# Second product with gathers: GpSimd's low parts start after the next group's weights, and VectorE's order is changed with them

## The chip, the cores and the metric

One NeuronCore of a Trainium2 chip runs the whole program. The engines are TensorE (PE), VectorE (DVE), ScalarE (ACT), GpSimd (POOL) and SyncE (SP, which only issues DMAs here). The metric is the device time of one execution in microseconds; lower is better.

## The reference, cut to what matters

The program is a two-layer block (attention and gated linear attention, then a recurrent layer), each layer followed by a PEER layer, a mixture of 16384 one-row experts. The change lies in the PEER layer of layer 0, in its last product.

```python
def peer_ffn(h, wq, k1, k2, u, v):
    ...                                   # scores, top 16 of 128 x 128 experts for each of 8 heads
    idx = jnp.take_along_axis(cand_i, pos, axis=-1)
    g = jax.nn.softmax(top_s, axis=-1).astype(h.dtype)
    def block(args):
        hb, ib, gb = args
        ue = jnp.take(u, ib, axis=0)
        ve = jnp.take(v, ib, axis=0)
        act = jax.nn.gelu(jnp.einsum('td,thkd->thk', hb, ue), approximate=False)
        return jnp.einsum('thk,thkd->td', gb * act, ve)
    out = lax.map(block, ...)             # 6 tiles of 128 tokens in layer 0, D = 1024
```

## The kernel before, in words

For 5 of the 6 tiles of 128 tokens in layer 0 the kernel does not gather: it has computed the activation of every expert for every token (`acts`) and a sparse matrix of gate values (`gates`), and the output is the dense product (acts * gates) times the table `peer_v`, 16384 rows by 1024 columns. The 6th tile is done with gathers: its 128 chosen rows of `peer_u` and of `peer_v` per token are fetched by indirect DMAs, multiplied and summed on VectorE. `combine_with_gathers` does both at once.

**Groups.** The table is cut into 128 slots of 128 rows, and four slots make a group (`GC = 4`, `NG = 32` groups). A group makes 10 **pieces** on TensorE (`NP = 10`: 5 tiles by 2 halves of 512 columns), each 12 matmuls: 4 slots by 3 products, since each operand is split into a high and a low fp16 part (`vh`, `vl` of the table, `wh`, `wl` of the weights) and the product of the two low parts is left out. The high and low buffers exist twice (index `q`), the loaded fp32 buffers `vr`, `gr`, `ar` once per slot `x` of a group. The result of a piece goes to one of 4 PSUM banks, and VectorE adds it into `ACC`; piece y + 4 may start when piece y has been added (`added`).

**The engines in a group.** All of it is one period per group g, in which the operands of group g + 1 are made while TensorE works on group g.
- VectorE (`period`, L1695) runs through the 10 pieces: for each the addition into `ACC` (L1700), and behind it what a table of numbers assigns to that piece (L1539): `weigh_at` the four products `ar = ar * gr` of group g + 1 (L1668), `low_at` the four subtractions `wl = ar - wh` of group g + 1 (L1673), `dot_at` the four row products with `ug` for the gathered tile (L1680), and `sum_at` the four additions of gathered rows `vg` into the PSUM tensor `sum_ps` (L1692), ahead of them `set_share` (L1685).
- ScalarE makes `vh` (L1626) from `vr` and `wh` (L1628) from `ar`, in the order vh0, wh0, vh1, wh1 and so on, then one gelu.
- GpSimd (`period`, L1593) makes the four `vl = vr - vh` of group g + 1 (L1591, function `low`), then issues four gathers of `ug` and four of `vg` (L1585), each when VectorE has finished with the buffer (`dotted`, `summed`).
- SyncE (L1576 to L1579) loads, slot by slot in this fixed order: `gr` and `ar` when `wl` of that slot of the group before is made (`w_cut`), then `vr` when its `vl` is made (`v_cut`). It waits at each step, so a later slot's loads stand behind an earlier slot's waits.
- TensorE (L1659) starts a group when its four `vl` (`v_cut`) and its four `wl` (`w_cut`) are made.

The operands of VectorE matter here. L1668 and L1673 read two tensors in SBUF, and so does the small L1685. L1700, L1680 and L1692 read one in SBUF and one in PSUM (`ex_R`, `hp`, `sum_ps`).

The function next door for layer 1 (`combine_experts`, matmuls on L1486) has no gathers, 8 PSUM banks and 8 pieces, and is not touched.

Of the kernel before, what the change touches and what calls it, by code (L numbers as in the profile page):

```python
# [1525 lines left out]
def combine_with_gathers(nc, io, gates, acts, chosen_rows, chosen_gates, HS, ACC, layer, first_tile):  # L1526
# [4 lines left out]
    GC = 4  # L1531
# [4 lines left out]
    SLOTS = PH * PTOP // NG  # L1536
    assert 2 * NP % BANKS == 0
    if NP == 10:
        weigh_at, low_at, dot_at, sum_at = (0, 0, 1, 1), (3, 3, 4, 4), (2, 2, 5, 5), (7, 8, 8, 9)  # L1539
    else:  # L1540
        weigh_at, low_at, dot_at, sum_at = (0, 0, 0, 0), (2, 2, 2, 2), (1, 1, 3, 3), (4, 4, 5, 5)
    with ExitStack() as c:
# [19 lines left out]
        with signals(nc, *names) as sems:  # L1562
# [6 lines left out]
            with nc.Block() as block:  # L1569
                @block.sync  # L1570
                def _(sp):
                    with sp.Fori(0, NG) as g:
                        for x in range(GC):
                            s = g * GC + x
                            sp.wait_ge(w_cut, s + 1)
                            sp.dma_start(gr[x][:, :], gates[bass.ds(s, 1), :, c0:c0 + NT].rearrange("o p t -> p (o t)")).then_inc(g_in[x], 16)  # L1576
                            sp.dma_start(ar[x][:, :], acts[bass.ds(s, 1), :, 0:NT].rearrange("o p t -> p (o t)")).then_inc(a_in[x], 16)
                            sp.wait_ge(v_cut, s + 1)
                            sp.dma_start(vr[x][:, :], v_src[bass.ds(s, 1)].rearrange("o p d -> p (o d)")).then_inc(v_in[x], 16)  # L1579

                @block.gpsimd
                def _(pool):
                    def gather(rows, ring, x, q, done):
                        pool.sem_inc(issuing, 1)
                        nc.gpsimd.indirect_dma_start(ring[x][:, :], None, rows,  # L1585
                                                     bass.IndirectOffsetOnAxis(ap=index[q][:, x:x + 1], axis=0)).then_inc(done[x], 16)

                    def low(g, q, x):
                        pool.wait_ge(v_high, g * GC + (x + 1))
                        pool.wait_ge(second_done, g * NP + NP)  # L1590
                        nc.gpsimd.tensor_tensor(vl[q][:, x, :], vr[x][:, :], vh[q][:, x, :], ALU.subtract).then_inc(v_cut, 1)  # L1591

                    def period(g, q):  # L1593
                        for x in range(GC):
                            low(g + 1, 1 - q, x)
                        pool.wait_ge(index_set, g + 2)
                        for x in range(SLOTS):
                            pool.wait_ge(dotted, g * SLOTS + (x + 1))
                            gather(u_rows, ug, x, 1 - q, ug_in)
                        for x in range(SLOTS):  # L1600
                            pool.wait_ge(summed, g * SLOTS + (x + 1))
                            gather(v_rows, vg, x, 1 - q, vg_in)

                    pool.sem_inc(v_cut, 4)
                    pool.wait_ge(index_set, 1)
                    for x in range(SLOTS):
                        gather(u_rows, ug, x, 0, ug_in)
                    for x in range(SLOTS):
                        gather(v_rows, vg, x, 0, vg_in)
                    for x in range(GC):  # L1610
                        low(0, 0, x)
                    with pool.Fori(0, NG // 2 - 1) as it:
                        period(it * 2, 0)
                        period(it * 2 + 1, 1)
                    period(NG - 2, 0)

                @block.scalar
# [378 lines left out]
def peer(nc, io, mods, dram, H, HS, hh, hl, ident, layer, first_tile, sparse, full, after=None, out=None):  # L1996

    scores, gates, acts = dram
    peer_scores(nc, io, hh, hl, scores, layer, first_tile)
    with ExitStack() as c:  # L2000
        chosen_rows = c.enter_context(nc.sbuf_tensor(f"chosen_rows{layer}", [P, PH * PTOP], I32)) if sparse else None
        chosen_gates = c.enter_context(nc.sbuf_tensor(f"chosen_gates{layer}", [P, PH * PTOP], F32)) if sparse else None
        choose_and_activate(nc, io, ident, hh, hl, scores, gates, acts, chosen_rows, chosen_gates, layer, first_tile, sparse, full)
        ACC = c.enter_context(nc.sbuf_tensor(f"ACC{layer}", [P, TILES, D], F32))
        if sparse:
            combine_with_gathers(nc, io, gates, acts, chosen_rows, chosen_gates, HS, ACC, layer, first_tile)
        else:
            combine_experts(nc, io, gates, acts, ACC, layer, first_tile)
        project_and_norm(nc, io, mods, H, ACC, None, list(range(first_tile, TILES)), layer, 1, f"n{layer}p", after, out)
# [120 lines left out]
```

## Time and profile before

| | us |
|---|---|
| median of 3 runs | 5429.59 (5426.74 to 5431.28) |
| the profiled execution's own time | 5424.05 |
| its span | 5422.3 |
| the stage of `combine_with_gathers`, first to last matmul (L1659) | 2319.7 to 3227 |
| busy over the span: PE / DVE / POOL / ACT | 4579.7 / 3673.8 / 1831.0 / 1468.3 |

How to read it. Times in the views count from the span's start. A line of the timeline gives start, duration, engine, line, operation, names and shapes, how many instructions it merges (x3), and in brackets the idle time of the engine before it with what ended that. Start to start is the true distance of two instructions; durations overlap by some 0.08 us. The view by windows gives for each stretch its length, then busy time and instructions (x) of PE, PEld (weight loads), DVE, ACT and POOL, the granted TensorE clock as a share of 2.4 GHz, the busy share of the 16 DMA engines, and GB/s. Matmul ends are modelled, so a busy PE is not yet PE at its pace; the pace is read from the distance of pieces. Some matmul records are missing, a few in a hundred.

### The profile page before, as it was taken

How to read it: one execution, taken by the hardware profiler on the slowest of the kernel's cores; microseconds unless marked ns; L12 is line 12 of the kernel's file. 1: busy time of each engine (PE TensorE's matmuls, PEld its weight loads, DVE VectorE, ACT ScalarE, POOL GpSimd, SP SyncE). 2: the span in 40 equal slices, each digit the busy share in tenths (PEclk: the TensorE clock that was granted, in tenths of full speed). 3: DMA queues.
4: the chain of work that ended last, by engine and by line, in shares of the span. 5: the costliest groups of instructions: out<-in, count | busy, mean ns of one | idle time of the engine just before them, and what ended most of it. 6: DMA issues, size and time to landing. Idle time of an engine off the chain costs nothing. (4 is left out here: it accounts for less than half of the span.)

```text
span 5422.3 us, 76669 instructions
## 1 busy us (share of the span) xinstructions
PE 4579.7 (84%) x24359; PEld 2373.7 (44%) x24359; DVE 3673.8 (68%) x10347; ACT 1468.3 (27%) x1798; POOL 1831.0 (34%) x956
## 2 busy tenths in 40 slices
PE   8687755698999999789999974777899899899996
PEld 1244534365555555434444432434455445344442
DVE  0213334506988988889899976962787896388886
ACT  0002222003333333322222212640333333323231
POOL 0120000242222222255655545405323333445453
PEclk9797867899999999999999996888999999999998
DMA  8200000123445435577787861122344554665553
GB/s 361 90 32 14 7 1 1 71 90 128 132 141 178 149 126 177 180 305 307 309 322 310 311 238 38 48 82 75 129 147 149 186 163 139 223 214 193 213 193 117
DMA packets 416203, 852.22 MB, mean 157 GB/s; under 512 B 30468, under 2 KB 199236, under 8 KB 411844
## 3 DMA queue, kind: packets, MB, share of 16 engines
q1 hardware_dynamic: 170792, 539.25, 27.9%
q10 hardware_dynamic: 208416, 177.30, 10.3%
q0 software_dynamic: 36864, 134.23, 6.3%
q8 instruction: 45, 0.74, 0.1%
q14 instruction: 86, 0.70, 0.0%
HBM read 686.99 MB, written 163.68 MB: 157 GB/s over the span
## 5 line engine op out<-in xcount | busy, mean ns | idle before, releaser
L1207 POOL TENSOR_TENSOR ca_ul<-ca_ur,ca_uh 128x1024 f16<-128x1024 f32 x256 | 546.9, 2136 | 1371.4 <-ACT ca_uh L1249 1371.4
L1218 PE MATMUL ca_A<-hh,ca_uh 128*128 128x512 f16 (+1 forms) x3072 | 851.2, 332 | 120.8 <-POOL ca_ul L1207 120.8
L1218 PE MATMUL ca_A<-hl,ca_uh 128*128 128x512 f16 (+1 forms) x3072 | 849.5, 331 | 0.0
L1218 PE MATMUL ca_A<-hh,ca_ul 128*128 128x512 f16 (+1 forms) x3072 | 847.4, 331 | 0.0
L1659 PE MATMUL ex_R<-ex_vh,ex_wh 128*128 128x512 f16 x1280 | 492.7, 385 | 93.1 <-DVE ACC L1700 48.9
L1659 PE MATMUL ex_R<-ex_vl,ex_wh 128*128 128x512 f16 x1280 | 491.4, 384 | 0.0
L1659 PE MATMUL ex_R<-ex_vh,ex_wl 128*128 128x512 f16 x1280 | 491.1, 384 | 0.0
L1461 POOL TENSOR_TENSOR ex_vl<-ex_vr,ex_vh 128x1024 f16<-128x1024 f32 x128 | 323.1, 2550 | 342.7 <-ACT ex_vh L1470 342.7
L1395 DVE TENSOR_SCALAR ca_hot<-ca_iota,ca_cur 128x128 f16<-128x128 f16 (+1 forms) x1152 | 422.2, 367 | 5.1
L1218 PEld LDWEIGHTS ca_A<-hh,ca_uh 128*128 128x128 f16 x3072 | 262.0, 100 | 369.7 <-issue 77.7
L1396 DVE TENSOR_SCALAR ca_hot<-ca_iota,ca_cur 128x128 f16<-128x128 f16 (+1 forms) x1152 | 420.4, 365 | 0.0
L1486 PE MATMUL ex_R<-ex_vh,ex_wh 128*128 128x512 f16 x1024 | 389.0, 380 | 24.4 <-DVE ex_wl L1501 24.4
L1256 ACT ACTIVATE ca_ga<-ca_A 128x640 f32<-128x640 f32 (+1 forms) x256 | 166.5, 650 | 828.3 <-PE ca_A L1218 827.9
L1486 PE MATMUL ex_R<-ex_vl,ex_wh 128*128 128x512 f16 x1024 | 388.9, 380 | 0.0
L1486 PE MATMUL ex_R<-ex_vh,ex_wl 128*128 128x512 f16 x1024 | 388.9, 380 | 0.0
L1218 PEld LDWEIGHTS ca_A<-hh,ca_ul 128*128 128x128 f16 x3072 | 262.3, 99 | 250.5 <-issue 15.8
L1218 PEld LDWEIGHTS ca_A<-hl,ca_uh 128*128 128x128 f16 x3072 | 262.6, 100 | 239.9 <-issue 16.5
L1351 DVE SCALAR_TENSOR_TENSOR ca_match<-ca_iota,ca_posf,ca_ci 128x64 f32<-128x64 f16 x1280 | 349.8, 340 | 2.8
L1591 POOL TENSOR_TENSOR ex_vl<-ex_vr,ex_vh 128x1024 f16<-128x1024 f32 x128 | 276.8, 2179 | 129.0 <-ACT ex_vh L1626 128.2
L1249 ACT ACTIVATE ca_uh<-ca_ur 128x1024 f16<-128x1024 f32 x256 | 269.6, 1053 | 168.9 <-issue 84.3
L1668 DVE TENSOR_TENSOR ex_ar<-ex_ar,ex_gr 128x640 f32<-128x640 f32 x128 | 219.7, 1737 | 94.9 <-DMA ex_ar<-acts 94.6
L1497 DVE TENSOR_TENSOR ex_ar<-ex_ar,ex_gr 128x512 f32<-128x512 f32 x128 | 202.0, 1635 | 108.1 <-DMA ex_ar<-acts 107.7
(335 smaller groups left out, 7930.4 us busy)
## 6 DMA issues: line engine op xcount, KB each, us to landing
ca_ur<-in_peer_u SPq DMA_DIRECT2D x256, 512.0 KB, 3.4
ex_vr<-in_peer_v SPq DMA_DIRECT2D x256, 512.0 KB, 6.6
gates<-ca_stage ACTq DMA_DIRECT2D x36, 2048.0 KB, 10.6
mod_w<-in_mod_w SPq DMA_DIRECT2D x12, 4096.0 KB, 12.4
acts<-ca_ga ACTq DMA_DIRECT2D x128, 320.0 KB, 2.2
ex_gr<-gates SPq DMA_DIRECT2D x128, 320.0 KB, 15.5
ex_ar<-acts SPq DMA_DIRECT2D x128, 320.0 KB, 17.2
acts<-ca_ga ACTq DMA_DIRECT2D x128, 256.0 KB, 2.8
```

The costliest lines, as they stand in the source:

```text
L1207: nc.gpsimd.tensor_tensor(ul[j][:, :, :], ur[j][:, :, :], uh[j][:, :, :], ALU.subtract).then_inc(u_cut, 1)
L1218: last = nc.tensor.matmul(A[b][:, a:a + w], lhs[b][:, k, :], rhs[:, k, a:a + w], start=(k == 0 and x == 0), stop=(k == KD - 1 and x == 2))
L1249: nc.scalar.activation(uh[b][:, :, :], ur[b][:, :, :], ACT.Copy).then_inc(u_high, 1)
L1351: step.mark(nc.vector.scalar_tensor_tensor(match[:, k, :], iota[:, 0:CAND], posf[:, h, k:k + 1], ci[:, h, :], ALU.is_equal, ALU.mult, accu ...
L1395: nc.vector.tensor_scalar(hot[j][:, x, 0, :], row[:, :], w(0), None, ALU.is_equal)
L1396: last = nc.vector.tensor_scalar(hot[j][:, x, 1, :], row[:, :], w(1), w(2), ALU.is_equal, ALU.mult)
L1461: nc.gpsimd.tensor_tensor(vl[q][:, x, :], vr[x][:, :], vh[q][:, x, :], ALU.subtract).then_inc(v_cut, 1)
L1486: last = nc.tensor.matmul(R[(NP * q + y) % BANKS][:, :], lhs[q][:, x, o:o + P], rhs[q][:, x, h * 512:h * 512 + 512], start=(x == 0 and n = ...
L1497: nc.vector.tensor_tensor(ar[x][:, :], ar[x][:, :], gr[x][:, :], ALU.mult).then_inc(weighed, 1)
L1591: nc.gpsimd.tensor_tensor(vl[q][:, x, :], vr[x][:, :], vh[q][:, x, :], ALU.subtract).then_inc(v_cut, 1)
L1659: last = nc.tensor.matmul(R[(NP * q + y) % BANKS][:, :], lhs[q][:, x, o:o + P], rhs[q][:, x, h * 512:h * 512 + 512], start=(x == 0 and n = ...
L1668: nc.vector.tensor_tensor(ar[x][:, :], ar[x][:, :], gr[x][:, :], ALU.mult).then_inc(weighed, 1)
```

## The change

GpSimd's `period` gets a wait ahead of its four `low`: it waits until all four `wl` of group g + 1 are made (`w_cut` at 4g + 12; `w_cut` starts at 4 and rises by four per group). VectorE's table for 10 pieces changes: the `wl` of group g + 1 move from pieces 3, 3, 4, 4 to 2, 2, 3, 3, and the dot products from 2, 2, 5, 5 to 4, 4, 5, 5. Nothing is added to or taken from the work.

```diff
     if NP == 10:
-        weigh_at, low_at, dot_at, sum_at = (0, 0, 1, 1), (3, 3, 4, 4), (2, 2, 5, 5), (7, 8, 8, 9)
+        weigh_at, low_at, dot_at, sum_at = (0, 0, 1, 1), (2, 2, 3, 3), (4, 4, 5, 5), (7, 8, 8, 9)
...
                     def period(g, q):
+                        pool.wait_ge(w_cut, g * GC + (2 * GC + 4))
                         for x in range(GC):
                             low(g + 1, 1 - q, x)
```

The order of VectorE in a period before, here in the last period that has a following group, from its fifth addition back to the dot products; ex_ar and ex_gr are the weights' factors, ex_wl their low part, ex_ug the gathered rows:

```order
1170 L1700 TENSOR_TENSOR ACC<-ACC,ex_R 128x512
1171 L1673 TENSOR_TENSOR ex_wl<-ex_ar,ex_wh 128x640 x2
1172 L1700 TENSOR_TENSOR ACC<-ACC,ex_R 128x512
1173 L1680 SCALAR_TENSOR_TENSOR ex_ug,ex_dot<-ex_ug,ex_hp 128x1024 x2
1174 L1700 TENSOR_TENSOR ACC<-ACC,ex_R 128x512 x2
1175 L1685 TENSOR_TENSOR ex_share<-ex_dot,chosen_gates 128x4
```

The same places of VectorE's order now:

```order
1170 L1701 TENSOR_TENSOR ACC<-ACC,ex_R 128x512
1171 L1681 SCALAR_TENSOR_TENSOR ex_ug,ex_dot<-ex_ug,ex_hp 128x1024 x2
1172 L1701 TENSOR_TENSOR ACC<-ACC,ex_R 128x512
1173 L1681 SCALAR_TENSOR_TENSOR ex_ug,ex_dot<-ex_ug,ex_hp 128x1024 x2
1174 L1701 TENSOR_TENSOR ACC<-ACC,ex_R 128x512 x2
1175 L1686 TENSOR_TENSOR ex_share<-ex_dot,chosen_gates 128x4
```

Behind the addition of piece 4 now stand dot products, where the last two `wl` stood; both pairs of `wl` are one piece earlier, and all four dot products lie behind them.

GpSimd in a period before (in brackets the semaphores waited for, by the name of their first user in the program: rows_in_0 is `v_high`, cond_in_0 `second_done`, prod0_0 `index_set`, prod1_0 `dotted`):

```order
107 L1589 ISA
108 L1590 ISA [waits rows_in_0]
109 L1591 TENSOR_TENSOR ex_vl<-ex_vr,ex_vh 128x1024 [waits cond_in_0]
110 L1589 REGISTER_ALU
111 L1591 TENSOR_TENSOR ex_vl<-ex_vr,ex_vh 128x1024 [waits cond_in_0,rows_in_0]
```

And now (silu_done_0 is `w_cut`):

```order
108 L1594 REGISTER_ALU
109 L1589 ISA [waits silu_done_0]
110 L1590 ISA [waits rows_in_0]
111 L1591 TENSOR_TENSOR ex_vl<-ex_vr,ex_vh 128x1024 [waits cond_in_0]
112 L1589 REGISTER_ALU
113 L1591 TENSOR_TENSOR ex_vl<-ex_vr,ex_vh 128x1024 [waits cond_in_0,rows_in_0]
```

The first `vl` of a group stands behind one wait more; behind it the order of GpSimd is the same: four `vl`, four gathers of `ug`, four of `vg`. SyncE, ScalarE and TensorE have the order they had.

## Rows read from the trace of the kernel before

**Rows 1.** View by windows: 100 us here, 100 us of layer 1's product.

```profile
2800.00:2900.00 100.00, 94.79 (x428) 41.59 (x427) 95.23 (x115) 24.72 (x32) 58.92 (x44) 0.98 0.84 326
5000.00:5100.00 100.00, 100.00 (x465) 45.36 (x464) 84.72 (x76) 31.53 (x40) 50.77 (x20) 1.00 0.56 197
```

**Rows 2.** Waits, 2320 to 3232 us: who for whom, total us, times, longest.

```profile
PEld ex_R L1659 <- DVE ACC L1700: 82.5, 64, 3.8
PE ex_R L1659 <- DVE ACC L1700: 48.9, 28, 3.3
DVE ex_ar L1668 <- DMA ex_ar<-acts: 76.6, 42, 3.8
```

**Rows 3.** Timeline of VectorE, three pieces that it had to wait for.

```profile
2328.01 0.69 DVE L1700 TENSOR_TENSOR ACC<-ACC,ex_R 128x512 f32<-128x512 f32 x1 [0.62 <-PE ex_R L1659]
...
3214.02 0.69 DVE L1700 TENSOR_TENSOR ACC<-ACC,ex_R 128x512 f32<-128x512 f32 x1 [1.61 <-PE ex_R L1659]
...
3224.38 0.69 DVE L1700 TENSOR_TENSOR ACC<-ACC,ex_R 128x512 f32<-128x512 f32 x1 [0.50 <-PE ex_R L1659]
```

**Rows 4.** Timeline of VectorE, one period and the next one's last product.

```profile
2809.53 0.68 DVE L1700 TENSOR_TENSOR ACC<-ACC,ex_R 128x512 f32<-128x512 f32 x1
...
2810.19 1.55 DVE L1668 TENSOR_TENSOR ex_ar<-ex_ar,ex_gr 128x640 f32<-128x640 f32 x2
...
2812.30 6.53 DVE L1668 TENSOR_TENSOR ex_ar<-ex_ar,ex_gr 128x640 f32<-128x640 f32 x1
2819.07 0.82 DVE L1668 TENSOR_TENSOR ex_ar<-ex_ar,ex_gr 128x640 f32<-128x640 f32 x1 [0.24 <-DMA ex_ar<-acts]
...
2823.29 2.65 DVE L1673 TENSOR_TENSOR ex_wl<-ex_ar,ex_wh 128x640 f16<-128x640 f32 x2
...
2826.46 1.55 DVE L1673 TENSOR_TENSOR ex_wl<-ex_ar,ex_wh 128x640 f16<-128x640 f32 x2
...
2838.36 0.68 DVE L1700 TENSOR_TENSOR ACC<-ACC,ex_R 128x512 f32<-128x512 f32 x1
...
2848.73 0.83 DVE L1668 TENSOR_TENSOR ex_ar<-ex_ar,ex_gr 128x640 f32<-128x640 f32 x1 [3.15 <-DMA ex_ar<-acts]
```

**Rows 5.** Timeline of GpSimd in the same period.

```profile
2811.84 6.29 POOL L1591 TENSOR_TENSOR ex_vl<-ex_vr,ex_vh 128x1024 f16<-128x1024 f32 x3
2822.39 2.13 POOL L1591 TENSOR_TENSOR ex_vl<-ex_vr,ex_vh 128x1024 f16<-128x1024 f32 x1 [4.25 <-ACT ex_vh L1626]
2824.66 1.36 POOL L1585 DMA_INDIRECT ex_ug<-in_peer_u_rows,ex_index  x1
```

**Rows 6.** By source line: instructions, duration ns min/median/max, first and last start.

```profile
L1668 DVE TENSOR_TENSOR ex_ar<-ex_ar,ex_gr x128: 812/824/6571, 2294.5 to 3188.6; 128x640 f32<-128x640 f32 x128
L1591 POOL TENSOR_TENSOR ex_vl<-ex_vr,ex_vh x128: 2116/2132/2732, 2303.2 to 3191.5; 128x1024 f16<-128x1024 f32 x128
L1700 DVE TENSOR_TENSOR ACC<-ACC,ex_R x320: 670/678/689, 2325.2 to 3227.6; 128x512 f32<-128x512 f32 x160
L1680 DVE SCALAR_TENSOR_TENSOR ex_ug<-ex_ug,ex_hp x128: 1204/1211/1219, 2334.5 to 3218.4; 128x1024 f32<-128x1024 f32 x128
L1692 DVE SCALAR_TENSOR_TENSOR ex_sum<-ex_vg,ex_share,ex_sum x128: 1279/1285/1291, 2345.1 to 3228.2; 128x1024 f32<-128x1024 f32 x128
```

**Rows 7.** Timeline of SyncE: first load of a group, fourth slot's ex_ar.

```profile
2825.37 0.34 SPq L1576 DMA_DIRECT2D ex_gr<-gates  x1
...
2830.84 0.40 SPq L1577 DMA_DIRECT2D ex_ar<-acts  x1
```

**Rows 8.** DMA view, 2790 to 2840 us: issues, KB each, median us to landing.

```profile
ex_vr<-in_peer_v SPq DMA_DIRECT2D x8, 512.0 KB, 18.5
...
ex_ar<-acts SPq DMA_DIRECT2D x8, 320.0 KB, 17.4
```

**Rows 9.** View by windows, two stretches of 2 us in that period.

```profile
2806.00:2808.00 2.00, 2.00 (x11) 0.90 (x10) 1.97 (x3) 0.00 (x0) 1.15 (x2) 1.00 1.02 412
2822.00:2824.00 2.00, 1.88 (x10) 0.70 (x8) 2.00 (x4) 0.94 (x2) 1.61 (x1) 1.00 0.00 0
```

## The prediction

> **What bounds the kernel now.** I read the stage in this order: the view by windows, to see whether TensorE is at its pace; the waits, to see what it waits for; one period on the timelines of VectorE, GpSimd and SyncE, to see what fills the period; the DMA rows, to see what the loads allow.
>
> TensorE is not at its pace. In 100 us of this stage it starts 428 matmuls, in 100 us of layer 1's product 465, with matmuls of the same shape [rows 1]; and the granted clock is 0.98 here and 1.00 there. What it waits for is VectorE's addition into ACC, that is a free PSUM bank: 82.5 us on the weight load's row and 48.9 us on the matmul's (the same pauses, seen twice) [rows 2]. It never waits for operands in the steady part.
>
> The pace without pauses is in the last group, where VectorE has little else to do: additions that waited for TensorE stand at 3214.02 and 3224.38, four pieces apart, so 2.59 us a piece and 25.9 us a group [rows 3]. The addition at 2328.01 is piece 1 of group 0, the one at 3224.38 piece 8 of group 31, 317 pieces later. They took 896.4 us, 28.3 a group. At 2.59 us they take 821.0. So **75.4 us** is all that can be got here while TensorE does the same matmuls.
>
> VectorE fills its period: from the first addition at 2809.53 to the next period's at 2838.36 is 28.83 us, and in it one product that normally takes 0.82 us takes 6.53, a pair of low weights 2.65 where the next pair takes 1.55, and 0.24 us is a wait for a DMA [rows 4]. Without these 5.71 + 1.10 + 0.24 us its work is 21.8 us, under TensorE's 25.9. The long product starts at 2812.30, while GpSimd runs three low parts without a break from 2811.84 to 2818.13, and ends 0.7 us behind them; the long pair has the fourth low part (2822.39 to 2824.52) over its start [rows 4, 5]. By line, L1668 goes from 0.82 up to 6.57 us, while L1700, L1680 and L1692, with one operand in PSUM, never vary by more than 0.02 [rows 6]. So VectorE's instructions with two SBUF operands stand still while GpSimd subtracts, the others do not.
>
> The Trainium skill ("SBUF — State Buffer", section "SBUF: two separate sides") describes this as a lock that whoever starts first holds for the whole instruction. The trace agrees that VectorE stops, but it shows 6.53 us, three GpSimd instructions and not one.
>
> There is a second loop, and in every other period it is the later one: loads. The product of slot 3 waits 3.15 us for its ar at 2848.73 [rows 4], 76.6 us in all [rows 2]. SyncE asks for a group's loads from 2825.37 on, when the first low weight of the group before is made, and for ar of slot 3 5.5 us later [rows 7]; it lands 17.4 us after that [rows 8]. The queues then move 412 GB/s [rows 9]. A group's four slots are 4 x (320 + 320 + 512) KB, the eight gathers 8 x 512 KB by their shape, 8.9 MB together, or 22 us at that rate; and then DMA stands still until the next first low weight (0 GB/s at 2822) [rows 9]. The loop is thus 5.5 + 17.4 + about 5.5 us back to the low weights, 28.4 us. Both loops must shorten for a gain.
>
> **The change, part by part.** I count from t = 0, TensorE's first matmul of group g, at its own pace, piece y ready at 2.59(y + 1). An addition takes 0.60 us start to start, two products or low weights 1.5, two dot products 2.3 [rows 4, 6].
>
> *VectorE's order.* Addition 0 at 2.7, products 0 and 1 to 4.9; addition 1 at 5.3, products 2 and 3 to 7.4; addition 2 at 7.9, low weights 0 and 1 to 10.0; addition 3 at 10.5, low weights 2 and 3 to 12.6. ScalarE must have wh3 by 11.8: it gets product 3 at 7.4, vh3 and wh3 take 1.0 and 0.7, so 10.1. The dot products go to pieces 4 and 5, 13.0 to 17.9. Same work, 21.8 us in 25.9: nothing added on the path. The four banks let VectorE lag by four pieces, and the heaviest piece (8, with two row additions, 3.2 us) is 0.6 over TensorE's pace, made up at once.
>
> *GpSimd's wait.* Queued behind it are four low parts, then four and four gathers. The low parts now run 12.7 to 21.2 (4 x 2.13 [rows 6]). TensorE needs them at 25.9: **4.7 us of cover**; beyond that every microsecond is lost on each of 31 groups. In that stretch VectorE has only additions and dot products, which don't stop. set_share (two SBUF operands) comes behind addition 7, at 21.4, just clear of the low parts; if VectorE lags it may meet them for some 2 us, and its period would be 23.8, still under 25.9. (By the lock rule of the page at most one instruction's 2.1 us, by the 6.53 us row up to a whole run of low parts; neither changes the sum.) The products of the next group begin at 28.6, far behind. So the 5.71 and 1.10 us are gone in every period.
>
> *Gathers.* ug are now issued 21.3 to 26.3 and needed at 38.9; vg, each after its row addition (22.9 to 28.4), 26.6 to 31.4, needed from 46.7. GpSimd is then idle to 38.5. No cost.
>
> *Loads, the part that could cost.* SyncE's order is slot by slot, so the loads behind vr of slot 0 now wait for low parts that start late. gr and ar of slot 0 go at 9.2 (earlier than before by a piece, 2.6 us); vr0, gr1 and ar1 at 14.9; each next slot 2.13 us later; ar3 at 19.8, vr3 at 21.3. ar3 is 10.6 us behind the first low weight, against 5.5 now. From there: ahead of ar3, and with it, stand 3.5 MB from 14.9 on; with the queues to themselves until the ug gathers begin to move at about 22.5, 2.4 MB of it is moved (two microseconds given to start), the other 1.1 MB at half the rate takes 5.5, so ar3 lands near **28**, some 8 to 9 us after it was asked for. It is needed at 32.6, the product of slot 3, and 4.7 us later still without loss to TensorE. vr3 lands near 31; vh3 is due at 34.2. All 8.3 MB that follow 14.9 are through by 36 or 37, before the next loads matter. So the 17.4 and 18.5 us of now don't hold: they were the wait behind a burst in which everything is asked for at once.
>
> *Sum.* The period goes from 28.3 to 25.9, in all 317 x 2.59 = 821.0 instead of 896.4: **-75.4 us**. Start (first loads, cold first pieces) and tail are untouched: the last group has no following one. The span is 5422.3 and lies 1.75 below that execution's 5424.05, which lies 5.5 under the median; 5424.05 becomes 5348.7, and the median 5429.59 becomes **5354**. Bounds of this case: by layer 1's rate (465 matmuls, 2.58 us a piece) 3 us less, so 5351, and 5345 with the spread of the runs; 0.3 us of start-up at each group, 10 us more, 5364.
>
> **The rivals.**
>
> *Slower: the loads are later than they are needed.* If ar3 still took the 17.4 us of now, the loop would be 10.6 + 17.4 + 2.2 (product, addition, low weight) = 30.2 us, 1.9 more than 28.3, on 31 groups +59 us: **5488**. It decides at a landing time of 13.1 us (no loss) and 15.5 (no gain). For it: 17.4 is what the trace has. Against it: in the trace ar3 lands at 2819.07, about when the whole 8.9 MB are through (412 GB/s at 2806, 0 at 2822), so that time measures the burst, which the new wait takes apart; and the queues have 3.9 us to spare in a period.
>
> *In between:* it lands in some 14 us, or the gathers get more than half the rate, or low parts slip beyond 25.9 in some groups: period 27, -40 us, **5390**.
>
> *No change:* the stall of VectorE is replaced, 1 for 1, by waits for ar or by TensorE's wait for vl, **5430**. For it: every other period already ends on DMA. Against: the rest of the loop is shorter by the 2.65 us pair and by a piece with two dot products, which now stand behind the low weights.
>
> The page "SBUF — State Buffer" (section "A bandwidth-pool intuition that's wrong") of the Trainium skill gives HBM to one core as some 358 GB/s. By that figure 8.9 MB would take 24.9 us, and with the gap between ar0 and vr0 (9.2 + 1.6 to 14.9, 4 us) the loads would hold the period near 28.9: this is the mechanism of no change, and it would speak against the whole change.
> By the rows 412 GB/s are moved for many microseconds, with this very mix of loads, and the same gap leaves 22 + 4 = 26 us only if nothing overlaps it; the last gathers of a group do overlap it. I give the mechanism a chance of 2 in 100, within the 5 below.
>
> *It doesn't do what it says:* I see no way; w_cut at 4g + 12 is exactly the four low weights of group g + 1, and they don't depend on GpSimd.
>
> **How the numbers follow.** Forecast 5354 (5345 to 5364): 75 in 100. In between, 5365 to 5415: 12. No change: 5. Slower: 8. The range must leave out at most 20: 5345 to 5395 takes the forecast and most of the in-between. A measurement of this kernel tells 0.2%, 11 us, from no change. Faster 0.87, within 0.2% 0.05, slower 0.08.
>
> **What the profile after would show.** Right: about 465 matmuls per 100 us and clock 1.00 in the stage, last matmul near 3151; L1668 at 0.82 us without long ones; GpSimd idle ahead of each group's first low part, waiting for VectorE's wl, and all four low parts back to back; additions that wait for TensorE in every group; ar and vr landing in about 9 us. Wrong: TensorE waiting at a group's start for vl (cover of 4.7 us used up), or VectorE waiting for ar on each slot 3 with a landing time over 13 us, or set_share of several us. The weakest steps are the landing of ar3 and vr3, and that the three low parts that held VectorE hold nothing else.

## The result and the profile after

| | us |
|---|---|
| before, median of 4 runs | 5429.18 (5426.74 to 5431.28) |
| after, median of 4 runs | 5354.39 (5349.47 to 5356.28) |
| ratio | 0.9861, 95% interval 0.9844 to 0.9878 |

The change makes the kernel 1.4% faster, 75 us. The lines of the file behind the new wait have moved down by one: L1668 of before is L1669 now, L1673 is L1674, L1659 is L1660, L1680 is L1681, L1685 is L1686, L1700 is L1701; L1591, L1585 and SyncE's lines stand where they stood.

View by windows of after, the 100 us of [rows 1] and 100 us earlier:

```profile
2400.00:2500.00 100.00, 100.00 (x465) 45.35 (x464) 88.59 (x124) 26.39 (x35) 61.65 (x45) 1.00 0.88 338
2800.00:2900.00 100.00, 100.00 (x465) 45.30 (x463) 88.64 (x124) 24.92 (x33) 65.02 (x48) 1.00 0.91 346
```

465 matmuls in 100 us where there were 428, the same as in layer 1's product [rows 1], at a granted clock of 1.00 (2.4 GHz) instead of 0.98. TensorE does not stop here any more.

By source line of after (the columns of [rows 6]):

```profile
L1669 DVE TENSOR_TENSOR ex_ar<-ex_ar,ex_gr x128: 816/819/2232, 2293.1 to 3106.8; 128x640 f32<-128x640 f32 x128
L1674 DVE TENSOR_TENSOR ex_wl<-ex_ar,ex_wh x128: 806/819/2509, 2312.9 to 3110.9; 128x640 f16<-128x640 f32 x128
L1591 POOL TENSOR_TENSOR ex_vl<-ex_vr,ex_vh x128: 2119/2135/2482, 2301.6 to 3118.1; 128x1024 f16<-128x1024 f32 x128
L1686 DVE TENSOR_TENSOR ex_share<-ex_dot,chosen_gates x32: 155/1786/1824, 2341.8 to 3144.7; 128x4 f32<-128x4 f32 x32
```

The longest product took 6.57 us [rows 6]; now it takes 2.23, once, ahead of the first group. The last row is the one that came out otherwise than forecast: `set_share`, four columns wide, was to be "just clear" of the low parts, and takes 1.79 us in the median instead of 0.15.

Timeline of VectorE in after, one period (the answer to [rows 4]):

```profile
2815.72 0.68 DVE L1701 TENSOR_TENSOR ACC<-ACC,ex_R 128x512 f32<-128x512 f32 x1
2816.31 0.16 DVE L1677 COPY ex_index<-chosen_rows 128x4 int32 x1
2816.39 1.55 DVE L1669 TENSOR_TENSOR ex_ar<-ex_ar,ex_gr 128x640 f32<-128x640 f32 x2
2821.12 0.69 DVE L1701 TENSOR_TENSOR ACC<-ACC,ex_R 128x512 f32<-128x512 f32 x1 [3.19 <-PE ex_R L1660]
2821.73 1.55 DVE L1669 TENSOR_TENSOR ex_ar<-ex_ar,ex_gr 128x640 f32<-128x640 f32 x2
...
2823.80 1.55 DVE L1674 TENSOR_TENSOR ex_wl<-ex_ar,ex_wh 128x640 f16<-128x640 f32 x2
...
2825.87 1.55 DVE L1674 TENSOR_TENSOR ex_wl<-ex_ar,ex_wh 128x640 f16<-128x640 f32 x2
...
2834.29 1.80 DVE L1686 TENSOR_TENSOR ex_share<-ex_dot,chosen_gates 128x4 f32<-128x4 f32 x1
```

The four products and four low weights stand in pairs of 1.55 us, none held. GpSimd in the same period, its last gather and its low parts:

```profile
2819.05 0.94 POOL L1585 DMA_INDIRECT ex_vg<-in_peer_v_rows,ex_index  x1 [0.30 <-issue]
2827.67 8.41 POOL L1591 TENSOR_TENSOR ex_vl<-ex_vr,ex_vh 128x1024 f16<-128x1024 f32 x4 [7.67 <-DVE ex_wl L1674]
```

It pauses 7.67 us for `wl`, and runs all four low parts back to back to 2836.08; in [rows 5] they came as three and one. `set_share`, started at 2834.29, ends with the fourth.

Timeline of SyncE in after, first load of the group, `vr` of slot 0, `ar` and `vr` of slot 3 (the answer to [rows 7]):

```profile
2824.79 0.34 SPq L1576 DMA_DIRECT2D ex_gr<-gates  x1
...
2829.97 0.33 SPq L1579 DMA_DIRECT2D ex_vr<-in_peer_v  x1
...
2835.46 0.60 SPq L1577 DMA_DIRECT2D ex_ar<-acts  x1
2836.27 0.41 SPq L1579 DMA_DIRECT2D ex_vr<-in_peer_v  x1
```

`ar` of slot 3 is asked for 10.7 us behind the first load, not 5.5 us. And yet, by the waits of after from 2320 to 3160 us:

```profile
POOL ex_vl L1591 <- DVE ex_wl L1674: 205.3, 28, 8.3
DVE ACC L1701 <- PE ex_R L1660: 77.7, 40, 3.2
DVE ex_ar L1669 <- DMA ex_ar<-acts: 1.2, 1, 1.2
```

VectorE's 76.6 us of waiting for `ar` [rows 2] are 1.2, one single wait, and TensorE's for VectorE's additions are gone from the list. VectorE waits for TensorE 40 times instead.

### The profile page after: what moved, and what is told of

Same layout as the page of the kernel before. It is cut to its first block and busy times, and to the rows that moved or that the text cites. A ratio compares the mean times of both kernels' runs of the same rounds, so it can differ in the third digit from the quotient of the medians.

```text
span 5354.5 us, 76699 instructions
## 1 busy us (share of the span) xinstructions
PE 4557.9 (85%) x24359; PEld 2375.4 (44%) x24359; DVE 3589.2 (67%) x10347; ACT 1463.0 (27%) x1798; POOL 1804.8 (34%) x956
## 5 line engine op out<-in xcount | busy, mean ns | idle before, releaser
L1660 PE MATMUL ex_R<-ex_vh,ex_wh 128*128 128x512 f16 x1280 | 486.1, 380 | 40.8 <-DVE ex_wl L1674 40.8
L1660 PE MATMUL ex_R<-ex_vl,ex_wh 128*128 128x512 f16 x1280 | 486.0, 380 | 0.0
L1660 PE MATMUL ex_R<-ex_vh,ex_wl 128*128 128x512 f16 x1280 | 485.9, 380 | 0.0
L1591 POOL TENSOR_TENSOR ex_vl<-ex_vr,ex_vh 128x1024 f16<-128x1024 f32 x128 | 269.4, 2137 | 244.9 <-DVE ex_wl L1674 205.3
L1701 DVE TENSOR_TENSOR ACC<-ACC,ex_R 128x512 f32<-128x512 f32 x320 | 217.1, 683 | 91.6 <-PE ex_R L1660 77.7
```

Source lines behind the costliest of these rows:

```text
L1660: last = nc.tensor.matmul(R[(NP * q + y) % BANKS][:, :], lhs[q][:, x, o:o + P], rhs[q][:, x, h * 512:h * 512 + 512], start=(x == 0 and n = ...
L1701: nc.vector.tensor_tensor(part, part, R[(NP * q + y) % BANKS][:, :], ALU.add).then_inc(added, 1)
```

## The experiments

Twelve more kernels were run. "317 pieces" is the distance used in the prediction, from VectorE's addition of piece 1 of group 0 to that of piece 8 of group 31, read from the timeline of the profiled execution, and "period" is that over 31.7 groups. Both leave out the start and the rest of the program, and this helps: the part behind the stage's last matmul, which no edit touches, took from 2196 to 2210 us in these 14 profiled executions. Each ratio is to runs of before on the same chip; the medians of different rows can come from different chips, so kernels are compared by ratios and pieces.

| kernel | median us | ratio to before (95%) | 317 pieces | period |
|---|---|---|---|---|
| before | 5429.18 | | 896.4 | 28.28 |
| after | 5354.39 | 0.9861 (0.9844 to 0.9878) | 821.0 | 25.90 |
| wait alone | 5362.03 | 0.9874 (0.9858 to 0.9890) | 828.5 | 26.14 |
| order alone | 5452.89 | 1.0043 (1.0026 to 1.0060) | 920.6 | 29.04 |
| factor in PSUM | 5426.17 | 0.9999 (0.9989 to 1.0008) | 895.7 | 28.26 |
| late low weights | 5439.66 | 1.0030 (1.0014 to 1.0046) | 906.5 | 28.60 |
| factor in PSUM, new order | 5378.06 | 0.9905 (0.9888 to 0.9922) | 844.2 | 26.63 |
| factor in PSUM, no `gr` load | 5344.96 | 0.9847 (0.9830 to 0.9863) | 820.3 | 25.88 |
| collision kept, no `gr` load | 5385.80 | 0.9918 (0.9902 to 0.9935) | 860.7 | 27.15 |
| probe | 5354.41 | 0.9857 (0.9840 to 0.9873) | 821.0 | 25.90 |
| wait for the products | 5430.36 | 1.0004 (0.9995 to 1.0013) | 901.5 | 28.44 |
| low parts first | 5350.14 | 0.9849 (0.9835 to 0.9862) | 822.6 | 25.95 |
| gather, then low parts | 5427.77 | 1.0000 (0.9991 to 1.0010) | 895.4 | 28.24 |
| gather, pause, low parts | 5356.47 | 0.9870 (0.9853 to 0.9886) | 824.1 | 26.00 |

### The two parts of the change

**Wait alone**: the kernel after with the table of before.

```diff
-        weigh_at, low_at, dot_at, sum_at = (0, 0, 1, 1), (2, 2, 3, 3), (4, 4, 5, 5), (7, 8, 8, 9)
+        weigh_at, low_at, dot_at, sum_at = (0, 0, 1, 1), (3, 3, 4, 4), (2, 2, 5, 5), (7, 8, 8, 9)
```

> The new wait of GpSimd with VectorE's old table (low weights behind pieces 3, 3, 4, 4, dot products 2, 2, 5, 5). Theory (two loops, the collision and the loads): the low parts start a piece (2.6 us) later than in the changed kernel, about 15.2 to 23.7 on the scale of a 25.9 us group, 2.2 us ahead of the end; collisions with the products are gone; the first load goes at 11.8 and ar of slot 3 is asked for at 22.4 and lands about 9 us later, at 31 to 32, just ahead of the 32.6 where it is due. So TensorE still keeps its pace: 5354, at most 5365. Rival (the order is what gives the gain, since it shortens the load loop): 5400 or more, with waits for ar on slot 3.

It gives nearly all of the gain, 5362, and stays under the 5365 expected at most. The low weights are finished a piece later and the low parts run from 2838.06 to 2846.45, so TensorE now waits for them here and there:

```profile
PE ex_R L1660 <- POOL ex_vl L1591: 3.9, 5, 1.3
```

The new table is thus worth 7.5 us in the 317 pieces; the intervals of the two ratios overlap, and only the piece times, one profiled execution each, separate them.

**Order alone**: the kernel before with the new table and no wait.

> VectorE's new table without GpSimd's wait. Theory: the low parts again start as soon as their table rows are cast and meet the products; the load loop is a piece and two dot products shorter, so ar should no longer be late, but the stall of some 6 us a period stays and VectorE needs 27 to 28 us: 5400 to 5425. Rival (order gives the gain): 5354 to 5370.

This is slower than before, and above the 5400 to 5425 that were expected. Timeline of VectorE, then of GpSimd, in it:

```profile
2824.93 7.30 DVE L1668 TENSOR_TENSOR ex_ar<-ex_ar,ex_gr 128x640 f32<-128x640 f32 x2
2832.76 3.48 DVE L1673 TENSOR_TENSOR ex_wl<-ex_ar,ex_wh 128x640 f16<-128x640 f32 x2
```

```profile
2824.52 6.29 POOL L1591 TENSOR_TENSOR ex_vl<-ex_vr,ex_vh 128x1024 f16<-128x1024 f32 x3
2833.30 2.26 POOL L1591 TENSOR_TENSOR ex_vl<-ex_vr,ex_vh 128x1024 f16<-128x1024 f32 x1 [2.49 <-ACT ex_vh L1626]
```

The low weights, now straight behind the products, meet the fourth low part in every period: 5.75 + 1.93 us are lost where it was 5.71 + 1.10 [rows 4] and a pair of dot products, which GpSimd does not hold, used to stand in between. VectorE is busy for all of the period (99.72 of the 100 us from 2800 to 2900) and sets it. Bringing VectorE's work forward without moving GpSimd's makes the collision larger. This kernel also speaks against a rival that is easily thought of, TensorE's clock: the granted clock over the stage is 1.00 here (2.4 GHz) and 0.98 in before, and yet it is the slower of the two.

### The two loops, each by itself

**Factor in PSUM**: the kernel before, with the products' second operand taken from PSUM (`hp`, so the gate factor is missing from the output), and one wait more at VectorE's start.

```diff
-                        nc.vector.tensor_tensor(ar[x][:, :], ar[x][:, :], gr[x][:, :], ALU.mult).then_inc(weighed, 1)
+                        nc.vector.tensor_tensor(ar[x][:, :], ar[x][:, :], hp[:, 0:NT], ALU.mult).then_inc(weighed, 1)
```

> The kernel before, in which the products of combine_with_gathers take hp (in PSUM) in place of gr as their second operand, so that they have one SBUF operand; gr is still loaded and waited for. This leaves the gate factor out of the output. Both theories: no product longer than 0.9 us any more, although the low parts run at the same places. If the collision alone held the period: TensorE's pace, about 5355. By my reading (the load loop is as long): ar of slot 3 still lands 21 to 22 us after the first load and the low weights come 5 us behind it, so 27 us a period, 5380 to 5400, with all of the remaining loss in waits for ar.

The products' collision is gone and the time stays (some low weights still meet the fourth low part, 14 us in the whole stage). All products take 0.82 us; VectorE waits for `ar` instead, 188 us in the stage where it was 76.6 [rows 2]:

```profile
L1668 DVE TENSOR_TENSOR ex_ar<-ex_ar,ex_hp x128: 806/815/823, 2293.6 to 3187.0; 128x640 f32<-128x640 f32 x128
```

```profile
2816.74 0.82 DVE L1668 TENSOR_TENSOR ex_ar<-ex_ar,ex_hp 128x640 f32<-128x640 f32 x1 [5.94 <-DMA ex_ar<-acts]
...
2845.79 0.82 DVE L1668 TENSOR_TENSOR ex_ar<-ex_ar,ex_hp 128x640 f32<-128x640 f32 x1 [5.96 <-DMA ex_ar<-acts]
```

The group's first load is asked for at 2822.36, and the product of slot 3 starts when its `ar` lands, 2845.79, 23.4 us later; from the product before it, 2816.74, to that first load it was 5.6 us. That is 29.0 in this period and 28.3 in the mean of all, where the prediction had added up 28.4. I had still expected a gain here, 5380 to 5400, taking the loop to be shorter without the stall; it is not.

**Factor in PSUM, new order**: the same with the new table.

> The kernel before with both: products with one SBUF operand (hp in PSUM in place of gr, which leaves the gate factor out of the output, gr still loaded) and VectorE's new table; GpSimd has no new wait. The run with the PSUM factor alone stayed at 5426 (its load loop is 28.7 us), the new table alone went to 5453 (its VectorE stalls 7.7 us a period and has no waits for ar). Theory (two independent loops, each enough to hold 28 to 29 us): with both shortened the period falls to TensorE's 25.9, or to about 26 since the low weights can still meet low parts (1.9 us a period): 5354 to 5365. Rival (the gain needs GpSimd's wait, since it takes the burst of loads apart): 5400 or more.

This is two thirds of the way, 52 of the 75 us in the pieces, and neither the 5354 to 5365 of the theory nor the 5400 of its rival. The low weights still read two SBUF tensors, and in 23 periods one of them is now held to the end of the low parts:

```profile
2837.17 6.88 DVE L1673 TENSOR_TENSOR ex_wl<-ex_ar,ex_wh 128x640 f16<-128x640 f32 x2
```

**Factor in PSUM, no `gr` load**: old table; `gr` is neither loaded nor waited for, 1.3 MB of 8.9 a group less. The gate factor is missing from the output here and in the next kernel.

> The kernel before, old table, no new wait; products with hp in PSUM as second operand, and gr is not loaded at all (gate factor left out of the output). A group then moves 7.6 MB in place of 8.9, 3.2 us less at 412 GB/s. Theory: collision of the products gone and the load loop at 28.7 - 3.2 = 25.5 us: TensorE's pace, 5354 to 5365. Rival (not the amount of the burst but its order or SyncE's sequence holds the loop): 5420.

Both loops are shortened without the change, and the period is TensorE's pace. The median is 9 us below that of after and of the range expected, with intervals that overlap; the first matmul comes 5.7 us earlier (2312.4 for 2318.1), presumably since the first loads are shorter too, and the part behind the stage 6.9 us less in the profiled execution (2198.7 for 2205.6), which no edit touches.

**Collision kept, no `gr` load**: the same, but the product reads `ar` twice from SBUF.

> As the run without gr, but the products take ar twice (two SBUF operands), so that they can meet the low parts. gr not loaded, output without the gate factor. Theory: the collision loop alone holds the period: VectorE 21.8 us of work and some 6 to 7 us of stall, 28 to 29 us: 5415 to 5440, with no waits for ar. Rival (the loads are what matters, the stall only fills the time in which VectorE would wait for them): 5354 to 5370.

```profile
2812.24 7.31 DVE L1666 TENSOR_TENSOR ex_ar<-ex_ar 128x640 f32<-128x640 f32 x2
```

The stall of 5.76 us is back, waits for `ar` are 0.4 us in all, and the period is 27.15. So the collision alone is worth 1.25 us a period above TensorE's pace, and the loads alone 2.4 (factor in PSUM). The loads are thus the longer of the two loops: taking away the collision alone gives nothing, while lighter loads with the products' collision kept give 46 us against before on the same chip. I had expected 5415 to 5440; the low weights, which start late enough in this kernel to meet no low part in all but two periods, were counted as hit.

### How late GpSimd may begin

**Late low weights**: the kernel after, dot products at pieces 2 and 3, low weights at 4 and 5.

```diff
-        weigh_at, low_at, dot_at, sum_at = (0, 0, 1, 1), (2, 2, 3, 3), (4, 4, 5, 5), (7, 8, 8, 9)
+        weigh_at, low_at, dot_at, sum_at = (0, 0, 1, 1), (4, 4, 5, 5), (2, 2, 3, 3), (7, 8, 8, 9)
```

> The changed kernel with low weights behind pieces 4, 4, 5, 5 and dot products behind 2, 2, 3, 3. The low parts then start at 17.9 and end at 26.4, 0.5 us after TensorE would need them, and the loads go 5.2 us later than in the changed kernel (ar of slot 3 at 25.0). Theory: the cover of 4.7 us is gone, TensorE waits for vl or VectorE for ar in every period, 0.5 to 1.5 us: 5370 to 5400. If there was more cover than I counted: 5354. If the loads behave as before the change (17 us to landing): 32.8 us or more a period, 5550.

```profile
PE ex_R L1660 <- POOL ex_vl L1591: 60.2, 31, 3.5
```

Two pieces later, 5.2 us, is more than the cover of the low parts (4.7 us in the prediction, 2.4 in fact, as shown below): TensorE waits for them in each of the 31 groups (the row is that of 2320 to 3220 us). The gain of 75 us becomes a loss of 10. The pieces take 85.5 us more than in after: 60.2 are these waits, and most of the rest, an estimate of 18 us, is slower matmuls, since the granted clock over the stage is 0.98, part of it at 1.2 GHz, where after has 1.00 (2% of 906.5 us). That is worse than the 5370 to 5400 expected; I had put the low parts' lateness at 0.5 to 1.5 us a group, and it is 1.9, with the clock on top.

### What holds VectorE, and for how long

**Probe**: the kernel after, with a small multiplication of two SBUF operands on VectorE behind the addition of piece 4.

> The changed kernel with one small instruction more on VectorE behind the fifth addition of each period: 4 columns, two SBUF operands, its result not used. It comes about 1 us after GpSimd began its four low parts. If the low parts hold VectorE's second operand for the whole run: it takes about 7.5 us, VectorE needs 29.3 us a period less what set_share no longer waits, and the time is some 90 to 110 us over the changed kernel, 5445 to 5465. If they hold it for one instruction each: at most 2.1 us, hidden in VectorE's spare 4 us, 5354.

```profile
2827.73 1.88 DVE L1710 TENSOR_TENSOR ex_probe<-chosen_gates 128x4 f32<-128x4 f32 x1
```

```profile
2827.47 8.40 POOL L1592 TENSOR_TENSOR ex_vl<-ex_vr,ex_vh 128x1024 f16<-128x1024 f32 x4 [7.63 <-DVE ex_wl L1675]
```

It ends at 2829.61, with the first of the four low parts (2827.47 + 2.13), in all 31 periods (1.39 to 1.90 us), while the others run on behind it. Here the hold is one GpSimd instruction long.

**Wait for the products**: the kernel after, GpSimd waits for the four products instead of the low weights.

```diff
-                        pool.wait_ge(w_cut, g * GC + (2 * GC + 4))
+                        pool.wait_ge(weighed, g * GC + 2 * GC)
```

> The changed kernel, but GpSimd waits only for the four products of the next group (weighed), not for its low weights, so that its four low parts start at about 7.5 on the scale of a group and the low weights of VectorE come while they run. If a run of low parts holds VectorE throughout: the low weights wait until about 16, the loads go after them, and the loop is 23.4 (burst) + 0.8 + 0.3 + 8.5 + 0.8 = 33.8 us a period: 5550 to 5600. If each low part holds it for itself alone: low weights get in between them, loop about 27 to 28: 5400 to 5430.

By source line:

```profile
L1674 DVE TENSOR_TENSOR ex_wl<-ex_ar,ex_wh x128: 806/2560/2747, 2314.5 to 3196.7; 128x640 f16<-128x640 f32 x128
L1591 POOL TENSOR_TENSOR ex_vl<-ex_vr,ex_vh x128: 2121/2705/2716, 2303.2 to 3196.1; 128x1024 f16<-128x1024 f32 x128
```

The two engines take turns: each low weight waits for one low part (2.56 us instead of 0.82), and each low part behind it is 0.57 us longer by a low weight. Four times 1.75 us are 7 us a period, as dear as one hold of 5.7 and one of 1.1, and the time is that of before. A wait is not enough; it has to be the right one.

That left a contradiction: one low part here, three in [rows 4, 5]. I went through all periods of these kernels, for each VectorE instruction of over 1.4 us that started inside a low part with another one straight behind it. What sorts them is what stands **ahead** of the run of low parts on GpSimd. With a gather ahead, without a pause, VectorE waited past the low part it had met in all 114 cases (30 in before, 30 with the order alone, 30 with the collision kept, 23 and 1 in the two kernels with the factor in PSUM that have any), 108 times to the end of the run, and six times, all in before, to the end of the second of three. With a pause ahead of the run it waited for one low part in all 140 cases. The gather of before is this row, 0.02 us ahead of [rows 5]:

```profile
2810.42 1.40 POOL L1585 DMA_INDIRECT ex_vg<-in_peer_v_rows,ex_index  x1 [0.85 <-issue]
```

Two kernels test it. **Gather, then low parts**: the probe kernel with the gather of the last `vg` moved behind the wait, directly ahead of the low parts, and the probe behind the addition of piece 5.

```diff
                         pool.wait_ge(w_cut, g * GC + (2 * GC + 4))
+                        gather(v_rows, vg, SLOTS - 1, q, vg_in)
                         for x in range(GC):
                             low(g + 1, 1 - q, x)
...
-                        for x in range(SLOTS):
+                        for x in range(SLOTS - 1):
                             pool.wait_ge(summed, g * SLOTS + (x + 1))
                             gather(v_rows, vg, x, 1 - q, vg_in)
```

> The kernel after, with a small operation on VectorE (128x4, two operands in SBUF, a probe whose result is not used) behind its addition of piece 5, about 3 us after the low weights are finished, and with the last gather of vg moved from the end of GpSimd's group to directly ahead of the four low parts, behind the same wait. Why do VectorE's instructions stand still through up to three low parts before the change, in the order-alone and in the factor-in-PSUM kernels, and through one in the probe and in the wait-for-products kernels? Counted over all periods, the long ones have a gather directly ahead of the run of low parts and the short ones a pause of GpSimd. Theory A (the hold is kept through a run that follows a gather without a pause): the probe comes in the first low part (about 1.4 to 3.5 us) and ends behind the last, 6 to 7 us, and VectorE's work of 21.8 us becomes over 28 us: some 5410 to 5440 us. Theory B (the gather has nothing to do with it; it depends on the operation or on where in a low part VectorE arrives): the probe takes under 2.3 us and the time stays that of the kernel after, 5350 to 5362.

GpSimd, then the probe by source line:

```profile
2817.95 0.94 POOL L1586 DMA_INDIRECT ex_vg<-in_peer_v_rows,ex_index  x1 [9.19 <-DVE ex_wl L1678]
2818.91 8.37 POOL L1592 TENSOR_TENSOR ex_vl<-ex_vr,ex_vh 128x1024 f16<-128x1024 f32 x4
```

```profile
L1713 DVE TENSOR_TENSOR ex_probe<-chosen_gates x31: 6553/6768/6780, 2339.5 to 3188.6; 128x4 f32<-128x4 f32 x31
```

**Gather, pause, low parts**: the same, with one wait more behind the gather.

```diff
                         gather(v_rows, vg, SLOTS - 1, q, vg_in)
+                        pool.wait_ge(dotted, g * SLOTS + 2)
```

> The same as the kernel with the gather directly ahead of the low parts, but GpSimd waits between them for VectorE's second dot product, a pause of about 1 us. The probe stands at the same place. Theory A: the pause ends the hold, the probe waits for one low part, at most 2.2 us, and the time is that of the kernel after, 5350 to 5365. Theory B: no difference from the kernel without the pause, whatever that shows.

```profile
2829.69 0.93 POOL L1586 DMA_INDIRECT ex_vg<-in_peer_v_rows,ex_index  x1 [6.10 <-DVE ex_wl L1679]
2832.02 8.40 POOL L1592 TENSOR_TENSOR ex_vl<-ex_vr,ex_vh 128x1024 f16<-128x1024 f32 x4 [1.39 <-DVE ex_ug L1686]
```

```profile
L1714 DVE TENSOR_TENSOR ex_probe<-chosen_gates x31: 1709/1884/1910, 2337.9 to 3118.5; 128x4 f32<-128x4 f32 x31
```

The same probe of four columns takes 6.77 us behind a gather and 1.88 behind a pause, in each of 31 periods, and the kernel takes 5428 or 5356 us. Both came out as theory A had it.

### Low parts first

The kernel after, with the four low parts of group 0 ahead of the first eight gathers.

> The changed kernel, with GpSimd's first four low parts (group 0) ahead of the first eight gathers. In the changed kernel the first loads (4.7 MB) share the queues with 4.2 MB of gathers and TensorE's first matmul of the stage comes at 2318.1, 41 us after its last one. Theory: the first loads land some 8 to 10 us earlier, but the gathers then stand in front of group 1's loads, whose low parts may be up to 7 us late once: in sum 2 to 9 us faster than the changed kernel, 5345 to 5352; no change if what TensorE waits for there is not the loads.

TensorE's first matmul comes at 2309.6 us instead of 2318.1, 8.5 us earlier; the 317 pieces take 1.6 us more. The median is 4 us below that of after, with intervals that overlap (0.9835 to 0.9862 and 0.9844 to 0.9878): a likely small gain that this comparison does not prove.

## Why the prediction was right, point by point

**The sum.** 317 pieces were to take 821.0 us instead of 896.4. They took this (timeline of VectorE in after, piece 1 of group 0 and piece 8 of group 31):

```profile
2325.69 0.69 DVE L1701 TENSOR_TENSOR ACC<-ACC,ex_R 128x512 f32<-128x512 f32 x1
...
3146.72 0.69 DVE L1701 TENSOR_TENSOR ACC<-ACC,ex_R 128x512 f32<-128x512 f32 x1 [0.50 <-PE ex_R L1660]
```

821.03 us. The last matmul starts at 3148.9, forecast "near 3151". The median came out at 5354.4, forecast 5354. Part of that closeness is luck: the profiled span fell by 67.8 us, not 75.4, since the part behind the stage took 2205.6 us in this execution and 2195.7 in that of before. It varies by as much among kernels that do not touch it.

**Two loops, both to be shortened.** Right in that both exist and that TensorE's pace needs both shortened: the load loop alone gives 28.26, the collision alone 27.15, both together 28.28. The load loop was added up as 28.4 us and measured 28.3. But "both loops must shorten for a gain" is right for one of them only. Without the collision nothing is gained; with lighter loads and the products' collision kept, 1.1 us a period are gained. The sum of VectorE's period as 21.8 + 5.71 + 1.10 us held only beside the load loop: with the lighter loads the low weights were no longer hit. For the forecast this made no difference, since the change shortens both.

**The loads.** `ar` of slot 3 was to be asked for at 19.8 and to land 8 to 9 us later. It is asked for 10.7 us behind the first load, as worked out (10.6). The DMA view gives no landing time for it. Its 16 completion signals are in the trace only in part, at most 6 of them in a period, and they come 6.0 to 9.7 us behind the asking (in before all 16 are there, the last 17.25 us behind it in the median); for `vr` of slot 3 it is 6.4 to 11.8 us. This fits the forecast without proving it. A firm bound: the wait for it is 1.2 us in the whole stage, and its product is the second of the pair 13 us behind the asking (asked 2808.64, pair started 2821.73), so it lands in under 14 us, not in 17.4. The rival "the loads are too late" fell. So did the mechanism of no change, which went by the 358 GB/s that the Trainium skill gives ("SBUF — State Buffer", section "A bandwidth-pool intuition that's wrong"). The period is 25.9 us and not 28.9, and the trace of after has 412 GB/s for 8 us (2838 to 2846) and 10 GB/s for 3 us (2828 to 2831), 338 and 346 on average over 100 us: the average is set by the pauses and not by the rate.

**VectorE's order and the cover of 4.7 us.** This step was off, at no cost. Counting 127 pieces of 2.59 us back from 3146.72, piece 1 of the group shown was complete at 2817.79, so that t = 0 of the prediction is 2812.61 here. The low weights end at 2827.4, t = 14.8, forecast 12.6; the low parts run from 15.1 to 23.5, forecast 12.7 to 21.2. The cover is **2.4 us**, half of what was put down. The 2.2 us are lost at one place, the addition of piece 1, which was to start at 5.3 and starts at 8.5 (2821.12), because of the late signal described at the end; part of it is caught up. `set_share` starts at 21.7 (forecast 21.4), and so meets the fourth low part and waits 1.8 us for its end: "just clear" was wrong, because the low parts were late, not because it was early. Both are hidden, as the sum had allowed: 21.8 + 1.8 us are still under 25.9. The experiments agree with the smaller cover: with the low weights one piece, 2.6 us, later TensorE just begins to wait (3.9 us in all), with two pieces later it waits in every group.

**"Additions that wait for TensorE in every group."** There are waits in 31 of 32 groups, but not for the reason forecast. VectorE has the slack that this was to show: the addition of piece 7 starts on the 2.59 us grid, to 0.05 us, in half of the groups. But much of the 77.7 us are the waits of 3 us at piece 1, which are something else.

**What held the 6.53 us.** The prediction set the rule of one instruction against its own row, which showed a whole run of low parts, and left both open, since neither changed its sum. Both happen. The row was not wrong; it was the case with a gather ahead. The Trainium skill ("SBUF — State Buffer", section "SBUF: two separate sides") says that whichever starts first "gets the pair for the whole instruction". The traces agree behind a pause (probe 1.88 us, set_share 1.80, low weights 2.56), and differ behind a gather (6.53, 6.77 us).

## What to carry to other kernels

When two engines share a way into SBUF, give them turns by a semaphore at the point where the one has no such instruction left for a while, and measure the cover behind it: here one piece (2.6 us) later cost a tenth of the gain, and two pieces later, or a wait one step too early, all of it. Before one stall is removed, look for the loop that would be next: here the collision could be taken away for nothing, and the order of VectorE changed alone for a loss. And a wait has a second effect: it decides what else is asked for at the same time. Here the gain needed both: taking away the products' collision by another operand left 28.26 us a period, and the wait alone, which also spreads the loads (10.4 us from a group's first load to `ar` of slot 3, where before has 5.5), gave 26.14.

## What the runs showed that was not expected

**A gather ahead lengthens the hold.** Up to four low parts, 6.8 us, against one, 1.9 us; a pause of 1.4 us in between is enough to end it. Why is open: whether it is the gather or the missing pause was not separated (a run behind another GpSimd instruction without a pause was not tried), nor how short the pause may be, nor whether such a pause alone would help the kernel before.

**A late signal.** In the kernel after, VectorE's addition of piece 1 starts 1.7 to 4.0 us behind the grid in 30 of 32 groups, 3.0 in the median, nearly always behind an idle wait for TensorE (3.19 us at 2821.12). Piece 2, due at 2820.38, is then added at 2823.20 without a wait, and piece 7 is back on the grid, so TensorE itself had not fallen behind: it starts 465 matmuls in 100 us. The trace's record of semaphores says a little more. All 28 waits of over 1 us at piece 1 end 0.02 us behind a completion signal of TensorE, and in 18 of them the next signal follows 0.12 us later, though a piece takes 2.59 us. So it is the signals of two finished pieces that come late and together, and not VectorE. The other kernels narrow it down: such waits of over 1 us stand 28 times in low parts first, 23 times in the probe kernel, 7 times in late low weights, 6 times in wait alone, 5 times with gather, pause, low parts, and once in factor in PSUM, no `gr` load, which runs at the same pace with lighter loads and without the wait. TensorE's pace alone does not bring them. What does was not found. The late signal took half of the cover of this change, and stays harmless only while four banks and 2.4 us are enough.
